# A hybrid decoder block with 32 experts: w_out in other ring slots, another order of the scan's units, half loads and half sums

## The chip, the cores and the metric

The kernel runs on 1 core of one Trainium2 chip. The metric is the device time of one execution in microseconds; the median of several is compared. All data is float32 unless a tile says bf16.

## The reference, cut to what matters

One layer on 256 tokens of width 1024. A norm and one wide projection feed a short convolution and an RWKV-7 scan; both are gated and merged, go through `w_out`, and a top-4-of-32 mixture of experts follows, then the last norm.

```python
p = rmsnorm(h, norm_mix_g) @ w_in                 # 1024 x 8480
y_conv = gb * conv3(gc * xin)
y_rwkv = rwkv7_time_mix(...)                      # 16 heads of 64, LoRA decay, head norms
h = h + (sigmoid(gate_conv) * y_conv + sigmoid(gate_rwkv) * y_rwkv) @ w_out
hn = rmsnorm(h, norm_ffn_g)
for e in experts:                                 # w1[e] 1024 x 2048, w2[e] 1024 x 1024
    h += gate_e * (clamped_swiglu(hn_e @ w1[e] + b1[e]) @ w2[e] + b2[e])
return rmsnorm(h, norm_final_g)
```

The scan is a recurrence over tokens of a 64 x 64 state per head with a decay, a rank-one removal and a rank-one addition per token. Heads' keys are normed: kk / max(|kk|, 1e-12).

## The kernel before, in words

**Memory.** `ring` has 16 slots of 2048 columns (1 MiB each). In the first part, slots 0 to 5 hold three double slots for chunks of `w_in` and `w_out` (`LOADS`, L251, gives the double slot of each of the 17 + 2 chunks), slots 6 to 10 K, KK, A, R and V, and 11 to 15 other arrays of the scan. The temporaries of the four lanes (64 tokens each) lie in `temps` (L125): one work array, slot 15, slot 4 and slot 5. In the expert part the ring is four groups of four slots (`GROUP`, L317). An expert takes three groups in turn: two for the halves of `exp_w1`, one for `exp_w2`, which is loaded in two halves.

**The queues.** SP (L374 on) issues the loads in program order. A chunk waits until the blocks of the chunk before it in its slot are projected (`blk_done`). An expert's loads (`load_expert`, L410) wait on `w_used`, which TensorE raises by 16 while it frees the slots of the first part (L862, L903, L910) and then by one for each slot used: 8 for `exp_w1`, 4 for `exp_w2` an expert. So an expert's first two groups wait for it * 12 + 4 and + 8, the halves of the third for + 10 and + 12. ACT issues the residual x (L1276) and some small loads.

**Order of work.** TensorE turns x (L459), projects blocks 0 to 66 (`project`, L480), each 8 x 2 records, and puts other work between blocks. In the first stage these are the LoRA products of the decay and of the in-context rate (`decay_and_iclr`, L498, after blocks 3 to 10), the head sums (`norm_sums`, L524, after block 11), their spread back over features (`norm_to_features`, L534, after block 13) and the gate's LoRA (L508). On VectorE the shift of each block (L1455), the prefix sum of the decay (L1479), its centring (L1488) and the norm's limit and reciprocal (L1490, L1494) stand in a fixed order.

From block 19 on comes the scan stage, an order written out by hand for TensorE (L742 to L859), ACT (L1189 to L1272) and VectorE (L1655 to L1789). The four lanes each build factors, invert a triangular matrix by a series and three merges (corner, joined, turn_e) and then pass through the state steps (z, u, y, s). `go` (L566) interleaves one or two units of 16 small products (64 x 64); a unit works either on the diagonal quadrants of the array or on the others, and `MERGE_AT` (L304) says which for the merges. Projections of the gates and of the convolution lie between, with copies, products and convolutions on ACT and VectorE (`gate_factor`, `take_gc`, `mix`, `convolve`, `gate_in`, `gate_conv`).

Then four out products (L866; t is the half of the tokens, half that of the columns), the turned residual for the router (L877), the choice of experts, and 32 experts (`expert`, L964): bias, eight slots of `exp_w1` (L983), the sum of the expert before (`combine`, L944), the gather for the next expert (L935), turns, four slots of `exp_w2` (L1018). At the end the last `combine`, the adds (L1898), and row by row the square sum and root on ACT (L1278), the reciprocal and the product with root and gain on VectorE (L1904), and the store (L443).

```python
pe.wait_ge(y_made, NCH)
pe.sem_inc(w_used, 8)
...
for n in range(NIN + 2):
    if n >= 3:
        sp.wait_ge(blk_done, blocks_until(buffer_before(n)))
```

Of the kernel before, what the change touches and what calls it, by code (L numbers as in the profile page):

```python
# [15 lines left out]
P = 128  # L16
# [62 lines left out]
def build(nc, x, w_in, w_out, norm_ffn_g, norm_final_g, w2, a2, g2, router_w, router_b,  # L79
          exp_w1, exp_b1, exp_w2, exp_b2, params, consts, out):  # L80
    with ExitStack() as ctx:
# [48 lines left out]
        gffn, gfin = flat(i_GB)[:, 1024:2048], flat(i_CS)[:, 0:1024]  # L130

# [18 lines left out]
        gfin_in = sem("gfin_in")  # L150
        merged = sem("merged")
# [99 lines left out]
        LOADS = [0, 1, 2, 0, 1, 2, 0] + [1, 0] * 6  # L251
# [52 lines left out]
        MERGE_AT = ((0, 1, 1), (1, 1, 0), (0, 0, 1), (0, 1, 0))  # L304
# [12 lines left out]
        GROUP = [8, 4, 12, 0]  # L317

        def group(u, j):

            return (3 * u + j) % 4
# [52 lines left out]
        def _(sp):  # L374
# [73 lines left out]
        def _(pe):  # L448
# [315 lines left out]
            go(series(0, 2), turn_v(0))  # L764
            go(f_rk(1), square(2))
            go(f_rb(2), series(1, 0))
            project(30)
            go(turn_e(0, 0), turn_b(0))
            go(series(2, 0), turn_v(1))
            go(series(1, 1), f_ak(2))  # L770
            go(turn_k(0))
            project(31)
            go(series(2, 1), f_rk(2))
            go(corner(0, 0), turn_b(1))
            project(32)
            go(turn_v(2), series(2, 2))
            go(turn_k(1), joined(0, 0))
            go(series(1, 2))
            go(turn_b(2), turn_e(2, 0))
            go(turn_e(0, 1))  # L780
            go(corner(0, 1))
            go(turn_k(2))
            project(33)
            go(joined(0, 1), corner(2, 0))
            go(turn_e(1, 0))
            go(corner(1, 0))
            go(turn_e(0, 2), joined(2, 0))
            project(34)
            go(joined(1, 0), turn_e(2, 1))
            go(corner(0, 2), corner(2, 1))  # L790
            project(35)
            go(joined(0, 2), joined(2, 1))
# [1140 lines left out]
```

## Time and profile before

| | us |
|---|---|
| median of 3 runs (lowest, highest) | 1344.51 (1344.16, 1347.29) |
| the profiled execution | 1345.06 |
| its span | 1343.3 |
| TensorE busy | 1234.8 (92%) |
| VectorE busy | 301.4 (22%) |
| ACT busy | 217.2 (16%) |
| GpSimd busy | 53.5 (4%) |
| DMA read, mean rate | 448.16 MB, 334 GB/s |
| chain that ended last | PE 63%, DMA 31%, DVE 3%, ACT 1%, issue 1% |
| waits of L983 for exp_w loads | 46.9 |

A span is the time from the first to the last record of the execution; what lies around it is 1.8 us here. Busy shares are means over stages with different limits: TensorE is busy nearly always, and its records in the expert part overlap with each other, so that share doesn't say that it sets the pace there. The chain follows each piece back to what released it. PE is TensorE's products, PEld its weight loads, DVE VectorE, POOL GpSimd. Line numbers are those of the kernel before.

### The profile page before, as it was taken

The numbers are of one execution on the slowest core, as the hardware profiler recorded it, in microseconds if no ns is written. First come the engines' busy times: TensorE is split into PE (matmuls) and PEld (weight loads), VectorE is DVE, ScalarE is ACT, GpSimd is POOL, SyncE is SP. The second block draws the span as 40 slices with busy tenths as digits, with TensorE's granted clock in tenths as the row PEclk, the third lists the DMA queues.
The fourth block names the chain that finished last, engine by engine and source line by source line (L and its number), as shares of the span: only waits on it lengthen the run. The fifth ranks groups of instructions, "written<-read, shape, count | busy, mean of one in ns | idle before, by whom it ended". The sixth has DMA issues, their size and how long they took to land.

```text
span 1343.3 us, 23536 instructions
## 1 busy us (share of the span) xinstructions
PE 1234.8 (92%) x10432; PEld 638.1 (48%) x10433; DVE 301.4 (22%) x597; ACT 217.2 (16%) x340; POOL 53.5 (4%) x32
## 2 busy tenths in 40 slices
PE   5989999999989999999999999899999989999996
PEld 4767888888744334333333333333333333343332
DVE  1254434233123112111112111111111111121112
ACT  4532221231032001100001100001110000110001
POOL 0700202000011000000000000000000000000000
PEclk9989999999988999999999999999999999999998
DMA  9421122333597999999999999999999999999993
GB/s 298 166 81 63 65 66 95 99 97 111 190 433 296 430 436 429 430 430 428 431 432 433 428 432 430 428 430 434 432 428 432 428 429 430 433 432 429 433 427 142
DMA packets 51620, 450.02 MB, mean 335 GB/s; under 512 B 5424, under 2 KB 23344, under 8 KB 35088
## 3 DMA queue, kind: packets, MB, share of 16 engines
q1 hardware_dynamic: 48576, 446.97, 80.0%
q10 hardware_dynamic: 2992, 2.25, 0.5%
q8 instruction: 46, 0.75, 0.2%
q14 instruction: 6, 0.05, 0.0%
HBM read 448.16 MB, written 1.05 MB: 334 GB/s over the span
## 4 chain that ended last, share of the span: by engine, by line
PE 63%; DMA 31%; DVE 3%; ACT 1%; issue 1%; ACTq 0%; SPq 0%; DVEq 0%
DMA ring<-in_exp_w 30%; PE ps L983 20%; PE ps L488 17%; PE ps L1018 10%; PE ps L573 4%; PE ps L949 3%; PE ps L940 2%; PE ps L873 2%; PE ps L575 1%; DMA ring<-in_w_out 1%; PE ps L996 1%; PE ps L973 1%; DVE work L1882 1%; PE ps L1005 1%; PE ps L506 0%
## 5 line engine op out<-in xcount | busy, mean ns | idle before, releaser
L983 PE MATMUL ps<-ring,work 128*64 128x512 f32 x2048 | 472.4, 617 | 46.9 <-DMA ring<-in_exp_w 46.9
L983 PEld LDWEIGHTS ps<-ring,work 128*64 128x64 f32 x2048 | 150.8, 142 | 351.2 <-issue 276.8
L488 PE MATMUL ps<-work,ring 128*128 128x256 f32 (+1 forms) x1120 | 244.1, 385 | 0.9 <-ACT work L1049 0.7
L1018 PE MATMUL ps<-ring,work 128*64 128x512 f32 x1024 | 225.1, 592 | 0.0
L488 PEld LDWEIGHTS ps<-work,ring 128*128 128x128 f32 (+1 forms) x1120 | 200.5, 186 | 34.6 <-issue 5.5
L1327 ACT ACTIVATE work<-work 128x512 f32<-128x512 f32 x32 | 20.1, 629 | 734.2 <-DVE work L1871 734.2
L1871 DVE TENSOR_SCALAR work<-ps 128x512 f32<-128x512 f32 x32 | 22.1, 692 | 500.0 <-PE ps L983 500.0
L1018 PEld LDWEIGHTS ps<-ring,work 128*64 128x64 f32 x1024 | 72.6, 137 | 129.5 <-issue 129.4
L1887 DVE COPY work<-ps 128x512 f32<-128x512 f32 x32 | 22.1, 691 | 208.2 <-PE ps L1018 208.2
L949 PE MATMUL ps<-work 64*128 64x512 f32 x264 | 65.6, 615 | 0.8 <-DVE work L1887 0.8
L940 PEld LDWEIGHTS ps<-sel,work 128*128 128x128 bf16 x1536 | 53.7, 118 | 24.2 <-issue 24.2
L940 PE MATMUL ps<-sel,work 128*128 128x64 bf16 x1536 | 57.1, 198 | 0.0
L573 PE MATMUL ps<-ring 64*64 64x64 f32 x1600 | 44.2, 220 | 2.1 <-issue 2.0
L949 PEld LDWEIGHTS ps<-work 64*128 64x128 f32 x264 | 22.8, 186 | 43.1 <-issue 41.5
L573 PEld LDWEIGHTS ps<-ring 64*64 64x64 f32 x1600 | 40.6, 135 | 4.9 <-issue 4.9
L1327 ACT ACT_TABLE_LOAD x32 | 41.1, 1283 | 2.1 <-issue 1.5
L873 PE MATMUL ps<-ring,work 128*128 128x512 f32 x64 | 30.0, 627 | 6.1 <-DMA ring<-in_w_out 6.1
L1329 ACT ACTIVATE work<-ps 128x512 f32<-128x512 f32 x32 | 19.1, 597 | 72.6 <-PE ps L940 72.6
L1005 PE MATMUL ps<-work,oh 96*64 96x512 bf16 x64 | 13.0, 403 | 16.5 <-DVE work L1882 16.5
L1461 DVE SCALAR_TENSOR_TENSOR ring<-ps,par,ring 128x255 f32<-128x255 f32 x24 | 11.5, 478 | 70.9 <-ACT ring L1066 70.7
L573 PE MATMUL ps<-cst,ring 64*64 64x64 f32 x768 | 25.2, 220 | 0.0
L1882 DVE COPY work<-ps 128x256 f32<-128x256 f32 x32 | 13.6, 424 | 50.8 <-PE ps L1000 50.8
(231 smaller groups left out, 733.0 us busy)
## 6 DMA issues: line engine op xcount, KB each, us to landing
ring<-in_exp_w SPq DMA_DIRECT2D x64, 4096.0 KB, 29.2
ring<-in_exp_w SPq DMA_DIRECT2D x64, 2048.0 KB, 30.0
ring<-in_w_in SPq DMA_DIRECT2D x8, 2048.0 KB, 8.3
ring<-in_w_in SPq DMA_DIRECT2D x16, 1024.0 KB, 6.7
ring<-in_w_out SPq DMA_DIRECT2D x2, 2048.0 KB, 10.3
ring<-in_w_in SPq DMA_DIRECT2D x1, 1152.0 KB, 7.3
work<-in_x SPq DMA_DIRECT2D x2, 512.0 KB, 4.1
work<-in_x ACTq DMA_DIRECT2D x2, 512.0 KB, 8.5
```

The source lines that it names most:

```text
L488: last = mm(bank_of(b)[width * g:width * g + width, 0:T], chunk(n)[:, k, c0:c0 + width], XN[:, k, :], start=k == 0, stop=k == KT - 1)
L573: last = mm(o, a(q, m), b_(q, m), start=True, stop=True)
L873: last = mm(ps[OUT[t][half]][:, :], Y[:, k, t * P:(t + 1) * P], chunk(NIN + half)[:, k, :], start=k == 0, stop=k == KT - 1)
L940: last = mm(ps[6][:, k * CAP:(k + 1) * CAP], H3[:, t, s, every_fourth(k)], sel[:, t, :], start=t + s == 0, stop=t + s == 3)
L949: last = mm(ps[2 * t + half][:, :], gts[64 * half:64 * half + 64, t * P:(t + 1) * P], yb[64 * half:64 * half + 64, :], start=False, stop=F ...
L983: last = mm(ps[4 + part][64 * half:64 * half + 64, :], xe[:, k * CAP:(k + 1) * CAP], ring[:, slot(u, k), part * D + half * 512:part * D + ...
L1005: last = mm(ps[7][64 * half:64 * half + 64, :], oh[:, :], b2s[:, half * 512:half * 512 + 512], start=True, stop=False)
L1018: last = mm(ps[7][64 * half:64 * half + 64, :], lhs, ring[:, slot(u, 8 + j), i * D + half * 512:i * D + half * 512 + 512], start=False, st ...
L1327: af(sig, glu, ACT.Sigmoid, scale=ALPHA).then_inc(sig_ready, 1)
L1871: ts(glu, ps[4][:, :], LIMIT, None, ALU.min).then_inc(glu_ready, 1)
L1882: cp(gts, ps[7][:, 0:T]).then_inc(gt_ready, 1)
L1887: cp(yb, ps[7][:, :]).then_inc(y_ready, 1)
```

## The change

Seven edits:
1. `w_out`'s two chunks go to slots 4, 5 and 2, 3 instead of 2, 3 and 0, 1. The first waits for the last merge of lanes 2 and 3, the second for chunk 15's blocks.
2. `GROUP` is [8, 12, 4, 0]; TensorE frees the second group when all four lanes are merged and the last two only after all four out products.
3. The table of the root is taken by a small root ahead of the first squares and ahead of the last ones; ACT's four small loads move behind the first root.
4. LoRA products in pairs; the norm's limit, ahead of the centring, and the root in block 11; shift(12) after the subtraction.
5. Another order of the units in the scan stage on three engines and another `MERGE_AT`; on GpSimd `first_e(2)` before `first_e(1)`. The same 118 units.
6. The second group of `exp_w1` of every second expert comes as two loads of two slots, each with a wait of its own.
7. The last sum is released per row half; the gain is multiplied ahead of the root, for one row on VectorE and for the other on GpSimd.

```diff
-        LOADS = [0, 1, 2, 0, 1, 2, 0] + [1, 0] * 6
+        LOADS = [0, 1, 2, 0, 1, 2, 0] + [1, 0] * 5 + [2, 1]
-        MERGE_AT = ((0, 1, 1), (1, 1, 0), (0, 0, 1), (0, 1, 0))
+        MERGE_AT = ((0, 1, 1), (0, 0, 0), (0, 1, 1), (0, 1, 0))
-        GROUP = [8, 4, 12, 0]
+        GROUP = [8, 12, 4, 0]
...
-                if n >= 3:
+                if n == NIN:
+                    sp.wait_ge(dve_e[2], 11)
+                    sp.wait_ge(dve_e[3], 11)
+                elif n >= 3:
                     sp.wait_ge(blk_done, blocks_until(buffer_before(n)))
...
+                    if (u, j) in half_in:
+                        rows_w1 = exp_w1[0, bass.ds(e, 1), 4 * P:8 * P, :].rearrange("a (p s) n -> p (a s) n", s=4)
+                        for half, done in ((0, group_in[group(u, j)]), (1, half_in[u, j])):
+                            sp.wait_ge(w_used, it * 12 + 6 + 2 * half)
+                            g0 = GROUP[group(u, j)] + 2 * half
+                            sp.dma_start(ring[:, g0:g0 + 2, :], rows_w1[:, 2 * half:2 * half + 2, :]).then_inc(done, 16)
+                        continue
...
-                if 3 <= b < 11:
+                if b in (4, 6, 8, 10):
+                    decay_and_iclr(b - 4)
                     decay_and_iclr(b - 3)
```

The scan stage on TensorE, its first third (the orders of ACT and VectorE follow it):

```diff
             project(23)
-            project(24)
-            project(25)
-            project(26)
             go(upper(0))
             go(lower(0))
+            project(24)
+            go(square(0), f_rb(0))
+            project(25)
+            go(upper(2), f_ak(0))
+            project(26)
+            go(f_rk(0), series(0, 0))
+            go(lower(2))
             project(27)
-            go(square(0))
-            go(upper(1), f_rb(0))
-            go(lower(1))
+            go(series(0, 1), f_rb(2))
+            go(turn_v(0), square(2))
+            go(upper(1))
+            go(lower(1), f_ak(2))
             project(28)
-            go(series(0, 0), f_ak(0))
-            go(upper(2), f_rb(1))
-            go(lower(2))
-            go(f_rk(0), square(1))
-            go(series(0, 1), f_ak(1))
+            go(square(1), f_rk(2))
+            go(series(2, 0), f_rb(1))
+            go(series(0, 2), turn_b(0))
...
```

Slots freed, the waits of an expert and the last sums:

```diff
             pe.wait_ge(y_made, NCH)
-            pe.sem_inc(w_used, 8)
+            pe.sem_inc(w_used, 4)
+            pe.wait_ge(merged, NCH)
+            pe.sem_inc(w_used, 4)
...
-            pe.wait_ge(merged, 4)
-            pe.sem_inc(w_used, 4)
             out_product(1, 0, 0, 8).then_inc(wout_done, 1)
...
             pe.wait_ge(wout_done, 2 * TT)
-            pe.sem_inc(w_used, 4)
+            pe.sem_inc(w_used, 8)
...
                 for k in range(8):
+                    if k == 6 and (u, 1) in half_in:
+                        pe.wait_ge(half_in[u, 1], turn_no * 16 + 16)
...
-            combine(n_rounds * E + 1)
+            pe.wait_ge(y_ready, n_rounds * E + 1)
+            for t in range(TT):
+                for half in range(2):
+                    last = mm(ps[2 * t + half][:, :], gts[64 * half:64 * half + 64, t * P:(t + 1) * P],
+                              yb[64 * half:64 * half + 64, :], start=False, stop=False, skip_group_check=True)
+                last.then_inc(last_sum, 1)
```

ACT, GpSimd and VectorE:

```diff
+            act.wait_ge(dve_chain, 1)
+            af(gn[:, 0, 0, 0:1], col[:, 31:32], ACT.Sqrt)
             for t in range(TT):
...
+            act.wait_ge(dve_rms, 1)
+            af(col[:, 4:6], col[:, 2:4], ACT.Sqrt).then_inc(act_rms, 1)
             mu_tail = P_AT["mu_lora"] + 2
             for g in range(4):
                 act.dma_start(col[32 * g:32 * g + 32, 40:41], params[0:32, mu_tail:mu_tail + 1],
                               allow_slow_non_contiguous=True).then_inc(mu_in, 16)
-            act.wait_ge(dve_rms, 1)
-            af(col[:, 4:6], col[:, 2:4], ACT.Sqrt).then_inc(act_rms, 1)
...
-                if b == 12:
+                if b == 11:
                     act.wait_ge(norm_max, 1)
                     af(nrm, nrm, ACT.Sqrt).then_inc(norm_root, 1)
...
+            af(gn[:, 0, 0, 0:1], col[:, 31:32], ACT.Sqrt)
             for t in range(TT):
                 root_of_squares(t, 16, 20, GC_rows, dve_h, 8 + t, act_h)
...
+            pool.wait_ge(dve_h, 9)
+            pool.wait_ge(gfin_in, 16)
+            ptt(HG[1], HB[:, 1, :], gfin, ALU.mult).then_inc(scaled_on_pool, 1)
...
-            shift(12)
             cs3 = flat(i_CS).rearrange("p (c t) -> p c t", t=HEAD)
-            link(tt(cs3, cs3, cm[:].rearrange("p m c -> p (m c)").unsqueeze(2).to_broadcast([P, NCH * KT, HEAD]), ALU.subtract))
             v.wait_ge(pe_sum, 1)
             ts(nrm, ps[4][:, 0:T], 1e-24, None, ALU.max).then_inc(norm_max, 1)
+            link(tt(cs3, cs3, cm[:].rearrange("p m c -> p (m c)").unsqueeze(2).to_broadcast([P, NCH * KT, HEAD]), ALU.subtract))
             link(tt(SW, CS, SW, ALU.subtract))
             v.sem_inc(dve_step, 1)
+            shift(12)
...
-            v.wait_ge(combined, n_rounds * E + 1)
+            v.wait_ge(gfin_in, 16)
             for t in range(TT):
+                v.wait_ge(last_sum, t + 1)
                 for half in range(2):
                     s_ = slice(512 * half, 512 * half + 512)
                     last = tt(HB[:, t, s_], HB[:, t, s_], ps[2 * t + half][:, :], ALU.add)
                 last.then_inc(dve_h, 1)
-            v.wait_ge(gfin_in, 16)
+            v.wait_ge(dve_h, 8)
+            link(tt(HG[0], HB[:, 0, :], gfin, ALU.mult))
             for t in range(TT):
                 v.wait_ge(act_h, 6 + t)
                 link(nc.vector.reciprocal(col[:, 22 + t:23 + t], col[:, 20 + t:21 + t]))
-                stt(HB[:, t, :], HB[:, t, :], col[:, 22 + t:23 + t], gfin, ALU.mult, ALU.mult).then_inc(out_ready, 1)
+                if t:
+                    v.wait_ge(scaled_on_pool, 1)
+                ts(HB[:, t, :], HG[t], col[:, 22 + t:23 + t], None, ALU.mult).then_inc(out_ready, 1)
```

## Rows read from the trace of the kernel before

**Rows 1.** Busy time by stretch: engines, then granted clock, DMA share, GB/s.

```profile
80.00:90.00 10.00, 7.43 (x36) 5.82 (x37) 4.87 (x4) 2.90 (x4) 0.00 (x0) 0.66 0.00 0
90.00:100.00 10.00, 9.24 (x46) 6.98 (x44) 5.81 (x11) 4.52 (x6) 0.00 (x0) 1.00 0.60 211
464.00:473.00 9.00, 9.00 (x48) 3.00 (x45) 0.89 (x2) 0.00 (x0) 0.00 (x0) 1.00 1.03 439
```

**Rows 2.** The timeline of the first norm: start, us, engine, line, idle before.

```profile
9.14 1.28 ACT L1046 ACT_TABLE_LOAD   x1 [2.16 <-issue]
...
10.67 0.17 DVE L1441 RECIPROCAL col<-col 128x2 f32<-128x2 f32 x1 [3.40 <-ACT col L1046]
...
10.87 1.42 DVE L1443 TENSOR_SCALAR ring<-work,col 128x1024 f32<-128x1024 f32 x2
```

**Rows 3.** The timeline of TensorE, the stage of the LoRA products and head norms.

```profile
31.73 0.70 PE L506 MATMUL ps<-work 64*128 64x256 f32 x4 [0.80 <-ACT work L1090]
...
71.04 7.07 PE L488 MATMUL ps<-work,ring 128*128 128x256 f32 x32
82.57 2.09 PE L540 MATMUL ps<-work,left 32*128 32x256 f32 x16 [4.46 <-DVE work L1494]
84.59 8.36 PE L488 MATMUL ps<-work,ring 128*128 128x256 f32 x32
```

**Rows 4.** The chain of waits in the scan stage: start, us, what.

```profile
204.29 2.02 PE ps L573 x128
...
225.97 1.09 PE ps L573 x64
227.07 3.65 PE ps L488 x16
```

**Rows 5.** The timeline of TensorE around the out products.

```profile
325.51 34.80 PE L488 MATMUL ps<-work,ring 128*128 128x256 f32 x160
...
373.23 15.93 PE L873 MATMUL ps<-ring,work 128*128 128x512 f32 x32 [6.05 <-DMA ring<-in_w_out]
...
389.87 7.03 PE L873 MATMUL ps<-ring,work 128*128 128x512 f32 x16
```

**Rows 6.** The timeline of VectorE around the head norms.

```profile
75.67 2.28 DVE L1488 TENSOR_TENSOR work<-work,cm 128x2048 f32<-128x2048 f32 x1
77.99 0.42 DVE L1490 TENSOR_SCALAR work<-ps 128x256 f32<-128x256 f32 x1
...
80.77 1.75 DVE L1494 RECIPROCAL work<-work 128x256 f32<-128x256 f32 x1 [0.15 <-DVE work L1491]
```

**Rows 7.** Who TensorE waited for up to 360 us: in total, times, longest.

```profile
PE ps L573 <- issue: 2.9, 4, 1.2
```

**Rows 8.** The timeline of SP: the first loads that wait for expert 0's end.

```profile
439.55 7.63 SPq L419 DMA_DIRECT2D ring<-in_exp_w  x2
```

**Rows 9.** The timeline of the last expert and the last norm.

```profile
1311.00 7.09 PE L983 MATMUL ps<-ring,work 128*64 128x512 f32 x32 [1.00 <-DMA ring<-in_exp_w]
...
1331.09 1.99 PE L949 MATMUL ps<-work 64*128 64x512 f32 x8 [0.80 <-DVE work L1887]
...
1333.13 2.48 DVE L1898 TENSOR_TENSOR work<-work,ps 128x512 f32<-128x512 f32 x4 [1.99 <-PE ps L949]
...
1335.61 1.28 ACT L1284 ACT_TABLE_LOAD   x1
...
1338.90 1.28 DVE L1904 SCALAR_TENSOR_TENSOR work<-work,col 128x1024 f32<-128x1024 f32 x1
```

**Rows 10.** DMA issues with us to landing: those of 420 to 421, of 439 to 440.

```profile
ring<-in_exp_w SPq DMA_DIRECT2D x1, 4096.0 KB, 13.6
...
ring<-in_exp_w SPq DMA_DIRECT2D x1, 4096.0 KB, 14.0
```

**Rows 11.** The timeline of GpSimd and VectorE while both work on SBUF.

```profile
405.46 2.13 POOL L1405 TENSOR_TENSOR left<-work 128x1024 f32<-128x1024 f32 x1 [6.44 <-DVE work L1843]
...
405.86 1.94 DVE L1848 SCALAR_TENSOR_TENSOR cnt<-cnt 128x1 f32<-128x1 f32 x2
```

More of the change, by code:

```diff
@@ L130, in build @@
         gffn, gfin = flat(i_GB)[:, 1024:2048], flat(i_CS)[:, 0:1024]
+        HG = (flat(i_CS)[:, 1024:2048], flat(i_GB)[:, 0:1024])
         const_in = sem("const_in")
@@ L766, in _ @@
[L766 removed]
+            go(turn_e(0, 0), turn_k(0))
+            go(f_ak(1), series(1, 0))
+            go(turn_v(2), series(2, 1))
             project(30)
[L768 to L771, printed above, removed]
+            go(corner(0, 0), turn_b(2))
+            go(series(2, 2), f_rk(1))
             project(31)
[L773 to L774 removed]
+            go(turn_v(1), joined(0, 0))
@@ L775, in _ @@
+            go(series(1, 1), turn_k(2))
             project(32)
[L776 to L782, printed above, removed]
+            go(turn_e(0, 1), series(1, 2))
+            go(corner(0, 1), turn_e(2, 0))
+            go(turn_b(1), corner(2, 0))
             project(33)
-            go(joined(0, 1), corner(2, 0))
@@ L802, in _ @@
+            project(38)
             go(joined(1, 2), f_ak(3))
-            project(38)
-            go(y_values(0), f_rk(3))
-            go(s_values(0), square(3))
-            go(z_values(0))
             project(39)
-            go(turn_v(3), series(3, 0))
-            go(u_product(0))
+            go(z_values(0), square(3))
+            go(s_values(0), y_values(0))
+            go(f_rk(3))
+            go(u_product(0), series(3, 0))
             project(40)
+            go(z_values(1), series(3, 1))
@@ L843, in _ @@
+            go(s_u(2))
+            project(53)
+            go(y_state(3), z_state(3))
+            project(54)
             go(u_product(3))
-            project(53)
+            project(55)
             go(y_u(3), turn_y(2))
-            project(54)
-            project(55)
             project(56)
-            go(turn_y(3))
             project(57)
@@ L1197, in _ @@
             scaled(19 + 4)
+            lower(0)
             scaled(19 + 5)
+            square(0)
             scaled(19 + 6)
             scaled(19 + 7)
-            lower(0)
+            lower(2)
             gate_factor(0)
-            square(0)
+            square(2)
+            turned(0, 0, V)
             lower(1)
@@ L1206, in _ @@
             square(1)
-            lower(2)
+            turned(0, 1, AA)
             gate_factor(2)
-            turned(0, 0, V)
-            square(2)
+            turned(0, 2, Kt)
+            turn_e(0, 0)
+            turned(2, 0, V)
             gate_factor(3)
-            turned(0, 1, AA)
-            turn_e(0, 0)
+            turned(2, 1, AA)
+            gate_factor(4)
             turned(1, 0, V)
-            turned(0, 2, Kt)
-            gate_factor(4)
+            turned(2, 2, Kt)
+            gate_factor(5)
+            turn_e(0, 1)
+            turn_e(2, 0)
             turned(1, 1, AA)
-            gate_factor(5)
-            turned(2, 0, V)
-            turned(1, 2, Kt)
-            turned(2, 1, AA)
-            turn_e(2, 0)
-            turn_e(0, 1)
-            turned(2, 2, Kt)
             gate_factor(6)
             turn_e(1, 0)
-            turn_e(0, 2)
+            turned(1, 2, Kt)
             gate_factor(7)
             turn_e(2, 1)
+            turn_e(0, 2)
             take_gc(0)
@@ L1233, in _ @@
             lower(3)
+            take_gc(1)
             turn_e(1, 2)
-            take_gc(1)
+            take_z(0)
             square(3)
-            take_z(0)
-            turned(3, 0, V)
             take_u(0)
@@ L1241, in _ @@
             square_y(0)
+            turned(3, 0, V)
+            root_y(0)
             turned(3, 1, AA)
-            root_y(0)
-            turned(3, 2, Kt)
             take_z(1)
@@ L1659, in _ @@
             shift(19 + 4)
+            upper(0)
+            lower(0)
             shift(19 + 5)
+            f_rb(0)
             shift(19 + 6)
+            f_ak(0)
+            upper(2)
             shift(19 + 7)
-            upper(0)
+            series(0, 0)
+            f_rk(0)
+            lower(2)
             v.wait_ge(hs_copied, 4)
```

180 lines of the change are left out of this document (87 added, 93 removed).

## The prediction

> **What bounds the kernel now.** I read the page first, then the chain of waits, then one stretch at a time by engine. The chain has two regimes. Up to expert 0 it is TensorE's own work, broken by a few waits. After that it runs through the loads of the expert weights: these keep the 16 DMA engines at about 430 GB/s and a full share, whichever weight is loaded (439 GB/s in a stretch of exp_w2) [rows 1]. 32 experts of 12.58 MB at that rate are 936 us, so most of the kernel can't be moved by reordering. What can move is what comes before the stream flows without gaps, and the tail after its last load. The stream holds only 16 slots. It fills once, then waits for expert 0 to use some. In that gap TensorE sets the time at which it resumes, so what TensorE gains ahead of expert 0 should reach the end one for one.
>
> **The first norm (ACT order and table).** Behind its squares (6.98) ACT issues four small DMAs (2.16 us) and then loads the table of the root (1.28 us) before the root itself can start, at 10.4, though VectorE had the mean ready 3.40 us before its next operation at 10.67, at 7.27 [rows 2]. After the change the table comes in while x is still on its way, and the DMAs stand behind the root: it starts at 7.3. All that follows is a chain into the transposes: 3.1 us won. The four DMAs are issued 0.5 us later and then take their 2.1 us of ACT's queue, which ends at 9.7; ACT's next work, the copies of the transposes, can't start before those scales of x (now 7.8 to 9.2) are turned. VectorE waits for them too, but shift(0) needs project(0) first.
>
> The Trainium skill (ScalarE: Activation LUTs, What ACT_TABLE_LOAD costs) adds about 1380 ns of drain to each load of 1283 ns. The trace differs: the load ends at 10.42 and VectorE has the root at 10.67. By the page this removal and the one in the tail would be worth 1.4 us more each.
>
> **LoRA in pairs.** TensorE waited 0.80 us for the sigmoids before its first LoRA product [rows 3]; now project(4) stands in between (3.6 us), so nothing is late there. Eight detours become four. A single projection in between costs 3.65 us, one of a row 34.80/10 = 3.48 [rows 4, 5], so each detour saved is worth 0.17: 0.7 us. Sum 1.5 us. The scan starts 0.6 us later, which fits before norm_sums ends.
>
> **Head norms ahead of the centring.** TensorE has two projections (7.07 us from 71.04, ending at 78.11) to cover the norm chain, but VectorE took the limit of the sums (0.42 us) only at 77.99, behind shift(12) and the centring of 2.28 us, and the reciprocal (1.75 us) at 80.77, so TensorE waited 4.46 us [rows 3, 6]. In the new order: sums done 71.2, limit to 71.7, root to 72.2 under the centring and the subtraction (2 x 2.28, to 76.2), shift(12) to 76.7, reciprocal to 78.5. TensorE waits 0.45 us instead of 4.46: 4.0 won. The two projections behind the wait then took 8.36 us where the two ahead of it took 7.07 [rows 3], and the granted clock of the stretch from 80 to 90 is 0.66, between its two levels of 1.2 and 2.4 GHz [rows 1]. Without the wait I take the fall away too: 1.3, and 0.1 less wait for gate_lora. Sum 5.4 us. ACT now waits for the limit inside block 11 with scaled(12) queued behind it, but that isn't due before 74.7.
>
> **The other unit order (scan stage).** I count units in the code. Each go() puts a diagonal and an off-diagonal unit on the array together, and a pair costs what a single costs: one go between projections is 1.09 us, two are 2.02 [rows 4], so 0.95 each and 0.15 a run. Before there are 69 gos (20 single) in 28 runs, after 65 (12 single) in 32 runs. 4 x 0.95 - 4 x (0.15 + 0.17) = 2.5 us less work. Waits between back-to-back gos were 2.9 us in 4 places [rows 7]. I followed each unit's operands through the new orders of VectorE and ACT: in most cases a projection stands between producer and user; the closest are turn_v(0) behind the bonus product and square(1) behind lower(1), with over 1 us to spare. I leave 0.3 us of waits: 2.6 won. Sum 5.1 us. Bounds: nothing (new waits eat the 4 gos; the orders of three engines moved at once) to 7.0.
>
> **w_out into the temporaries' slots.** The second half of w_out is loaded only after the last projection, beside the first two expert groups, and out_product(0, 1) waits 6.05 us for it. It then runs slowly: 15.93 us for two products, where one by itself takes 7.03, some 6.9 without the overlap at its ends [rows 5]. After the change its slots are those of chunk 15, free four projections (14 us) before the end; the first half goes to the temporaries of lanes 2 and 3 and is issued eight projections (28 us) before the end. At 350 GB/s (worked out below) its 2.1 MB need 6 us. SP's new wait for those two lanes is met when it gets there, since SP first waits for block 58. TensorE then goes through: from 360.3 four products and the turns between (0.7) are 28.3 us, against 36.6 (389.87 + 7.03 = 396.9). 8.3 won. The residual x, which ACT loads beside the expert groups, comes late for the first product as before, but its add is due only when the second product has ended, 7 us later.
>
> **Ring groups in another order.** The third group (exp_w2 of expert 0) and the fourth are now issued only after all four products, where the third had gone at 373.5. All above taken off (23.4), the products end at 373.5. Two groups of 4.19 MB need 22 us from there at 430 GB/s, to 396. Expert 0 was done at 439.55 [rows 8] and its exp_w2 calls are as many as one group of exp_w1 has, 7.09 us [rows 9], so they now begin at 409: hidden. Were that cover gone, it would cost at most the 13.6 us of a load on an empty queue [rows 10].
>
> **Half loads.** The refill is issued when expert 0 has used two slots instead of four: some 4 us sooner. But the load behind it and the two of exp_w2 waits until expert 0 is finished (439.55), and landed 14.0 us later, where the one issued on an idle queue took 13.6 [rows 8, 10]. So only 0.4 us reaches the stream; the rest becomes a gap. In the tail, TensorE waited just 1.00 us at the last expert's second group [rows 9]: the split gives that 1.0 and no more. Sum 1.4.
>
> **Sums per row half.** The first adds start behind two of the four calls, half of their 1.99 us sooner, and the table load of 1.28 us goes under the expert's work [rows 9]: row 0's root is ready 2.3 us sooner. VectorE then multiplies row 0 by the gain (1.28) while GpSimd does row 1 (2.13); each scale by the root is 0.71 (1.42 for two in the first norm) [rows 2]. Would they run side by side, the last scale ended 2.4 us sooner. But beside a GpSimd operation of 2.13 us two VectorE operations on one element each took 1.94 us, until GpSimd was done [rows 11]. VectorE's product starts first (from 1334.7 to 1336.0 on the old clock), so GpSimd's ends at 1338.1, and the last scale at 1338.9 instead of 1340.2: 1.3 won.
>
> The Trainium skill (SBUF — State Buffer, SBUF: two separate sides) says that a VectorE operation in a two-port mode, or with two SBUF inputs, and a GpSimd one lock each other out, whoever is first. The row agrees for two inputs; for a scale by a column no row shows it.
>
> **Sum.** 3.1 + 1.5 + 5.4 + 5.1 + 8.3 + 1.4 + 1.3 = 26.1 us. The profiled execution took 1345.06 (0.55 over the median of 1344.51), so 1319.0; the median of new runs may read half a microsecond lower.
>
> **The rivals.**
> Both scales wait for GpSimd: if row 0's scale is locked out like a two-input one, both run after 1338.1 and end at 1339.6: the tail gives 0.6, time 1319.7. This is the page's rule above.
> New waits in the scan stage: if the order loses what it saves in gos, 1324.1. For it: three orders interlock, and VectorE and ACT have table loads there. Against: the gaps of before stood where three and more gos followed each other, and there are fewer of those now.
> The w_out gain isn't passed on, because the two late groups hold up expert 0 or the stream: 1327.3. For: their issue moves behind the products. Against: 20 us of slack.
> More than forecast: no waits left in the scan (7.0) and a side-by-side tail (2.4): 1316.0.
> **Slower:** the halved loads read [p, 2, 2048] instead of one flat row. If they are cut in smaller pieces and run like w_in, 211 GB/s at a share of 0.60, so 350 at a full one [rows 1], the 67 MB of the 16 halved groups take 191 us instead of 156: +35 us, time 1354. It decides from 26 us on. Against: exp_w2's rows are half as long as exp_w1's and load as fast.
>
> **How the numbers follow.** Forecast 0.42, both scales wait 0.15, waits in the scan 0.20, w_out not passed on 0.08, more than forecast 0.10, slower 0.03, some mishap that leaves no difference 0.02. The range 1314.5 to 1328 takes in all cases that are faster, with 1.5 us below the best for clock falls that I priced too low. A measurement of this kernel tells 0.3% (4 us) from no change. Faster 0.95, same 0.02, slower 0.03.
>
> **What would show it.** Right: first transposes at 9.3; norm_to_features waits under 1 us; last projection ends near 345; no wait for in_w_out, and the four products take 28.3 us; expert 0 ends 23 us earlier, near 416; the refill's gap moves behind its w2 loads; no table load behind the last sums. Wrong: a stretch of halved loads under 420 GB/s, TensorE waits above 3 us between 130 and 300, or a second group of expert 0 or 1 that lands late.

## The result, and the profile after

| | us, median (lowest to highest) | profiled execution | its span |
|---|---|---|---|
| before | 1345.37 (1344.16 to 1347.29) | 1345.06 | 1343.3 |
| after | 1329.99 (1327.33 to 1332.31) | 1329.39 | 1327.6 |

The ratio is 0.9877, with an interval of 0.9863 to 0.9891: faster by 15.4 us, where 26.1 was forecast. The sign was right, the size was not: the time lies 2 us above the range.

To see where the gain went, I cut both traces at the same five events and compare the lengths of the pieces, in us.

| piece | before | after | won | forecast |
|---|---|---|---|---|
| start to the end of the head sums | 117.9 | 106.3 | 11.6 | 10.0 |
| scan, up to the first product of the output | 242.2 | 242.7 | -0.5 | 5.1 |
| the four products of the output | 36.8 | 34.2 | 2.5 | 8.3 |
| from there to expert 0 | 15.0 | 15.0 | 0 | 0 |
| expert 0 to the end of the last exp_w1 | 906.1 | 904.3 | 1.8 | 1.4 |
| the tail, to the end of the span | 25.2 | 25.0 | 0.2 | 1.3 |

Two pieces carry the miss. First the scan. The view of who TensorE waited for, from 104 to 365 us (in total, times, longest), after the change:

```profile
PE ps L588 <- issue: 5.5, 5, 2.2
```

It answers to [rows 7]: the saved gos are there, but there are 2.6 us more of waits that have no engine at their other end.

One pair of traces is a weak base for this. The traces of the experiments below include two more with the old order, and four more with the new order and nothing done against these waits: with all products of that window counted, the old order's waits on issue are 3.1 to 4.6 us (mean 3.9) in a scan of 242.2 to 243.6 (mean 243.0), the new order's 4.3 to 5.5 (mean 5.0) in one of 240.4 to 242.7 (mean 241.5). So the new order wins 1.5 us in the mean, not -0.5, still far from 5.1.

The longest wait, in the chain of waits of the changed kernel (start, us, what):

```profile
213.97 1.09 PE ps L588 x64
215.06 3.65 PE ps L502 x16
...
219.80 0.95 PE ps L590 x62
220.75 1.16 PE ps L588 x40
221.91 2.23 issue
224.14 1.76 PE ps L588 x54
225.90 4.32 PE ps L502 x16
```

The wait falls in the middle of a go, behind 40 of its small products, and the projection behind it takes 4.32 us where its neighbour takes 3.65. So TensorE does not seem to wait for an operand of a unit. What else moved just then shows in the view of the DMA engines from 205 to 230 us, in 40 slices (busy tenths, GB/s), with its queues:

```profile
DMA  0000000000000000779999999960000000000000
GB/s 0 0 0 0 0 26 0 0 0 0 0 0 26 0 0 0 75 224 370 388 378 369 352 349 347 342 185 0 0 0 0 0 26 0 0 0 0 0 0 0
q8 instruction: 4, 0.07, 1.0%
```

The lone slices of 26 GB/s are packets of the queue that the profile calls "instruction": 16 KB each, the lone ones 4 us apart or more. The load of w_in's chunk 11 fills the engines from 215 to 222 us, and the fourth such packet lies within it: in narrower windows it starts at 221.52 us and takes 1.07 us.

Second, the products of the output. The timeline of TensorE and of SP, after:

```profile
345.39 1.00 SPq L433 DMA_DIRECT2D ring<-in_exp_w  x2
...
349.02 20.76 PE L886 MATMUL ps<-ring,work 128*128 128x512 f32 x48
373.59 1.62 PE L896 MATMUL ps<-cst,work 128*128 128x128 f32 x8 [3.81 <-DVE work L1825]
375.00 8.23 PE L886 MATMUL ps<-ring,work 128*128 128x512 f32 x16
```

The 6.05 us for w_out of [rows 5] are gone: three products go through in 20.76 us. Then TensorE waits 3.81 us for the residual, and the last product takes 8.23 us; the granted clock from 374 to 376 us is 0.50, the lower of its two levels. VectorE had in turn waited for x, as the chain shows:

```profile
349.67 0.47 ACTq L1296
350.14 0.03 issue
350.17 22.06 DMA work<-in_x
372.25 1.30 DVE work L1825 x2
```

The DMA issues of the whole execution (KB each, us to landing) have x at 21.7 us:

```profile
work<-in_x ACTq DMA_DIRECT2D x2, 512.0 KB, 21.7
```

Before the change it was 8.5 us, and x was issued 0.3 us ahead of the expert groups, since SP had stood at w_out's second half until then (the same views of the kernel before):

```profile
346.53 14.18 SPq L391 DMA_DIRECT2D ring<-in_w_out  x2
360.81 1.03 ACTq L1276 DMA_DIRECT2D work<-in_x  x2
361.11 1.00 SPq L419 DMA_DIRECT2D ring<-in_exp_w  x2
...
work<-in_x ACTq DMA_DIRECT2D x2, 512.0 KB, 8.5
```

The tail, timeline of the last norm, answers to the end of [rows 9]:

```profile
1315.59 1.99 PE L1044 MATMUL ps<-work 64*128 64x512 f32 x8 [0.80 <-DVE work L1912]
...
1316.84 2.48 DVE L1924 TENSOR_TENSOR work<-work,ps 128x512 f32<-128x512 f32 x4 [1.20 <-PE ps L1044]
...
1319.40 3.26 POOL L1439 TENSOR_TENSOR work<-work 128x1024 f32<-128x1024 f32 x1 [918.32 <-DVE work L1924]
...
1320.69 2.52 DVE L1933 TENSOR_SCALAR work<-work,col 128x1024 f32<-128x1024 f32 x1
...
1323.31 0.75 DVE L1933 TENSOR_SCALAR work<-work,col 128x1024 f32<-128x1024 f32 x1
```

VectorE's scale of row 0 takes 2.52 us and ends 0.55 us after GpSimd's product; the same scale a moment later takes 0.75.

### The profile page after: what moved, and what is told of

Same layout as the page of the kernel before. It is cut to its first block, busy times and chain, and to the rows that moved or that the text cites. A ratio compares the mean times of both kernels' runs of the same rounds, so it can differ in the third digit from the quotient of the medians.

```text
span 1327.6 us, 23606 instructions
## 1 busy us (share of the span) xinstructions
PE 1223.7 (92%) x10433; PEld 642.8 (48%) x10433; DVE 304.0 (23%) x598; ACT 213.5 (16%) x339; POOL 58.9 (4%) x33
## 3 DMA queue, kind: packets, MB, share of 16 engines
HBM read 448.16 MB, written 1.05 MB: 338 GB/s over the span
## 4 chain that ended last, share of the span: by engine, by line
PE 62%; DMA 32%; DVE 3%; issue 1%; ACT 1%; SPq 0%; ACTq 0%; DVEq 0%
DMA ring<-in_exp_w 30%; PE ps L995 20%; PE ps L502 17%; PE ps L1030 10%; PE ps L588 4%; PE ps L959 3%; PE ps L950 2%; DMA work<-in_x 2%; PE ps L590 1%; PE ps L1008 1%; PE ps L983 1%; DVE work L1907 1%; PE ps L886 1%; PE ps L1017 1%; PE ps L1012 0%
## 5 line engine op out<-in xcount | busy, mean ns | idle before, releaser
L995 PE MATMUL ps<-ring,work 128*64 128x512 f32 x2048 | 465.1, 611 | 50.4 <-DMA ring<-in_exp_w 50.4
L995 PEld LDWEIGHTS ps<-ring,work 128*64 128x64 f32 x2048 | 159.0, 141 | 341.1 <-issue 286.8
L1030 PE MATMUL ps<-ring,work 128*64 128x512 f32 x1024 | 225.1, 592 | 0.0
L1030 PEld LDWEIGHTS ps<-ring,work 128*64 128x64 f32 x1024 | 72.5, 137 | 129.6 <-issue 129.5
L1439 POOL TENSOR_TENSOR work<-work 128x1024 f32<-128x1024 f32 x1 | 3.3, 3256 | 918.3 <-DVE work L1924 918.3
L1486 DVE SCALAR_TENSOR_TENSOR ring<-ps,par,ring 128x255 f32<-128x255 f32 x24 | 11.6, 482 | 60.2 <-ACT ring L1085 59.8
## 6 DMA issues: line engine op xcount, KB each, us to landing
work<-in_x ACTq DMA_DIRECT2D x2, 512.0 KB, 21.7
```

The lines of the kernel that those rows point to most:

```text
L995: last = mm(ps[4 + part][64 * half:64 * half + 64, :], xe[:, k * CAP:(k + 1) * CAP], ring[:, slot(u, k), part * D + half * 512:part * D + ...
L1030: last = mm(ps[7][64 * half:64 * half + 64, :], lhs, ring[:, slot(u, 8 + j), i * D + half * 512:i * D + half * 512 + 512], start=False, st ...
```

## The experiments

The theory after this reading had three parts. **x:** the expert groups, no longer behind w_out on SP, are issued 4 us ahead of x (345.39), and x, in 4 KB packets on ACT's queue, shares each DMA engine with their 32 KB packets. **Code:** TensorE runs dry of instructions where many small products follow one another, above all when a load has the DMA engines. **Tail:** VectorE is locked out by GpSimd. All ratios are to the kernel before, timed beside them (1345.8 to 1347.1 us); the changed kernel's was 0.9877 (0.9863 to 0.9891).

**1. Expert loads held until x has landed.**

```diff
+            sp.wait_ge(xres_in, 16 * TT)
             with sp.Fori(0, E // 4) as i:
```

> The changed kernel, but SP issues no expert load before the residual x has landed. Theory (x, issued on ACT's queue behind two expert groups already in flight, waits in each DMA engine behind their 32 KB packets): x lands within 6 us of its issue instead of 22, the four out products run through in 28.3 us instead of 34.1, and the time falls by 5.5 to 6 us to about 1324; the expert groups start some 9 us later, which costs nothing. Rival 1 (the x loads are slow by themselves, through their 4 KB rows or ACT's queue): x still takes some 20 us and the time does not move. Rival 2 (the expert stream is late already): the out products gain 5.8 us, but the first expert starts later or waits, and the time stays or grows.

1324.0 us (1322.55 to 1326.34), ratio 0.9825 (0.9805 to 0.9845). TensorE's timeline:

```profile
350.36 20.76 PE L887 MATMUL ps<-ring,work 128*128 128x512 f32 x48
370.96 1.04 PE L897 MATMUL ps<-cst,work 128*128 128x128 f32 x8
371.83 7.03 PE L887 MATMUL ps<-ring,work 128*128 128x512 f32 x16
```

x landed in 5.5 us, the wait and the slow product are both gone, and the four products take 28.5 us: the 28.3 of the prediction. The expert groups are issued 12 us later (357.80), where 9 was expected, and no wait for them comes of it: from the products to expert 0 it is 15 us in both traces.

**2. exp_w1 in pieces of 8 KB** (all its loads read "(s p)" instead of "(p s)", so the rows of W1 lie in another order and the output is another).

> The changed kernel with exp_w1 loaded in pieces of 8 KB instead of 32 and 16 KB (rows of exp_w1 so meet other features: the experts compute another sum, with the same amount of work). Theory (each packet of x waits for one expert packet on its engine): x has 16 packets of 4 KB per load and engine, 32 in all; with 8 KB packets of 0.3 us instead of 1.2 us it lands in 8 to 12 us instead of 22, soon enough for the second product, and the out products take 29 to 31 us. If x just shared the bandwidth by bytes, it would land at the same 22 us. The same kernel prices small pieces for the stream: if 8 KB pieces run as fast as 32 KB ones (430 GB/s), the expert stage stays at 904 us and the time falls by 3 to 6 us; if they cost 5%, 268 MB take 31 us longer.

1337.68 us (1336.0 to 1338.66), ratio 0.9929 (0.9909 to 0.995). With nothing held, x landed in 14.0 us and the products again took 28.5 us: how long x takes hangs on the size of the others' packets. That is later than the 8 to 12 us expected; x's two loads are 256 packets of 4 KB, so 16 for each engine and not 32. The price is in the stream, busy time by stretch (engines, clock, DMA share, GB/s), from 500 to 1200 us, first the changed kernel, then this one:

```profile
500.00:1200.00 700.00, 644.44 (x3964) 257.06 (x3960) 114.89 (x242) 73.67 (x96) 0.00 (x0) 0.98 1.00 430
```

```profile
500.00:1200.00 700.00, 636.04 (x3918) 255.17 (x3916) 113.86 (x240) 73.66 (x96) 0.00 (x0) 0.98 1.01 424
```

1.4% less, and the experts take 917.6 us instead of 905.8 in experiment 1. So the case of 430 GB/s and a gain of 3 to 6 us did not come.

**3. The load of chunk 11 held until block 41 of the scan.**

```diff
+                elif n == 11:
+                    sp.wait_ge(blk_done, 41)
                 elif n >= 3:
```

> The changed kernel, but the load of chunk 11 of w_in (214 to 222 us) is held until block 40 is projected. In the changed kernel TensorE stood 2.2 us at 221.9, within four gos in a row, with all operands there. Theory (its code is late: the gos use instructions faster than they are fetched, and the fetch shares the DMA engines with the load): the wait falls to 0.5 to 1 us, as at the other places without a load, the projection behind it runs at full clock, and the scan stage gets 1.5 to 2.5 us shorter. Rival (an operand or a semaphore): the wait stays at 2.2 us. If holding the chunk is too late, a wait for the ring appears before block 43 instead.

1327.8 us (1326.87 to 1329.25), ratio 0.9859 (0.9839 to 0.9879). The scan took 239.7 us instead of 242.7 (241.5 in the mean of the five traces above). By its time alone the gain is not clear of the noise, since the interval overlaps that of the changed kernel; the trace is clearer. Who TensorE waited for:

```profile
PE ps L590 <- issue: 3.2, 5, 1.4
```

The work and the order of the engines are the changed kernel's; only a load went elsewhere, and 2.3 us of waits with it. Between 205 and 240 us 0.5 us of them are left, of 2.2:

```profile
216.33 3.65 PE ps L504 x16
...
221.07 0.95 PE ps L592 x62
222.02 1.16 PE ps L590 x40
223.18 0.54 issue
```

TensorE stops behind the same 40 products, 6.85 us after the start of the same projection (216.33, in the changed kernel 215.06). But the instruction packet starts 4.80 us after it (221.13) instead of 6.46 (221.52): 1.66 us sooner without the load, and the wait is 1.69 us shorter. The packet itself takes as long, 1.12 and 1.07 us. Nor is it only this wait. In all 14 traces of this document, from the start of the small products to the products of the output, the chains have 71 waits on issue of over 0.15 us, and each of them ends 1.2 to 1.6 us after one of these packets has landed, while the packets themselves are mostly 4 us or more apart. The long wait stands in every trace of the new order in which nothing is done against it: 2.23, 2.23, 2.18, 2.18 and, on the kernel before, 1.95 us.

**4. The old scale at the end** (no product on GpSimd, VectorE's fused scale by root and gain as before; the half sums and the early table stay).

> The changed kernel with the last rows scaled as before (one VectorE operation of 1.28 us a row with root and gain, nothing on GpSimd), but sums per row half and the early table kept. Theory (GpSimd and VectorE lock each other out there, so the split of the scale costs more than it gives): from the last sums' first product to the end of the last scale 7.0 to 7.3 us instead of 8.5, and the time 1.2 to 1.5 us shorter. Rival (the tail is set by the stores): no gain.

1330.58 us (1328.12 to 1331.2), ratio 0.9872 (0.9851 to 0.9893): no difference that the median shows. In the trace the last norm is shorter:

```profile
1319.10 1.99 PE L1044 MATMUL ps<-work 64*128 64x512 f32 x8 [0.80 <-DVE work L1909]
...
1323.37 1.28 DVE L1926 SCALAR_TENSOR_TENSOR work<-work,col 128x1024 f32<-128x1024 f32 x1
...
1324.77 1.28 DVE L1926 SCALAR_TENSOR_TENSOR work<-work,col 128x1024 f32<-128x1024 f32 x1
```

From the last sums to the last scale 6.95 us, against 8.47 after and 9.09 before; the tail to the span's end 23.0, against 25.0. The tail is 23.0 to 23.1 us in all five traces with the old scale and half sums, and 25.0 to 25.1 in the five with the new one. What may hide it in the median is told with experiment 8.

**5. w_out's slots alone** (on the kernel before).

> The kernel before with one part of the change: both groups of w_out go into the temporaries' slots (with the ring groups in the other order and the wait of the loads that goes with them); norms, scan order, expert loads in 4 MB and tail stay as before. Theory (residual x is the limit once w_out is not): products of the output 34 us instead of 36.6, x 20 us or more from issue to landing, TensorE waits some 4 us for the centred residual, all together 1342.9 us. Rival 1 (the gain of 8.3 us that the prediction gave this part, x lands in time when nothing else is changed): products 28.3 us, 1337. Rival 2 (the part gives nothing by itself): 1345.4.

1344.43 us (1341.64 to 1346.94), ratio 0.9987 (0.9976 to 0.9999). x took 21.5 us, TensorE waited 3.61 us for the residual, and the products took 34.9 us: the late x comes with this part (w_out's place, the groups' order and their wait) and needs nothing else of the change. The time fell by 1.4 us against the kernel before beside it, half of the expected 2.9; this trace's head sums and scan are together 2.8 us longer than in the first trace of before, by the spread that is told above and with experiment 8.

```profile
362.97 20.76 PE L878 MATMUL ps<-ring,work 128*128 128x512 f32 x48
387.34 1.97 PE L888 MATMUL ps<-cst,work 128*128 128x128 f32 x8 [3.61 <-DVE work L1802]
389.10 8.77 PE L878 MATMUL ps<-ring,work 128*128 128x512 f32 x16
```

**6. The scan's order alone** (on the kernel before).

> The kernel before with another part of the change alone: the order of units, projections and sums in the scan, on all four engines. Theory (2.5 us of work are saved, but as much comes back as waits of TensorE with no engine late): scan from project 19 to the products of the output 242.4 to 243 us as before, TensorE idle on issue about 5.5 us in place of 2.9, 1345 to 1346 us together. Rival (the new waits belong to another part of the change, such as the other place of w_out): scan 240 us, idle on issue about 3, 1342.9 us.

1345.8 us (1342.57 to 1350.12), ratio 0.9994 (0.9979 to 1.0008). The time is as expected, the reason only in part: in the trace the scan was 1.8 us shorter (240.4), with 4.3 us of idle on issue, but w_out's second half, still loaded late, was waited for 6.20 us, and the products took 38.0 us instead of 36.8. So in this trace 1.3 us of the gain was lost again at the products; why they took longer than before is not shown.

**7. Projections 40 to 46 one place earlier** in TensorE's order (on the kernel after).

```diff
             go(s_values(0), y_values(0))
+            project(40)
             go(f_rk(3))
             go(u_product(0), series(3, 0))
-            project(40)
+            project(41)
             go(z_values(1), series(3, 1))
             go(y_u(0), s_u(0))
             go(turn_v(3))
-            project(41)
+            project(42)
...
```

> The kernel after, with projections 40 to 46 one place earlier in TensorE's order, so that the longest run of small products without a projection is cut in two. Theory (TensorE runs dry where a long dense run of small instructions uses up its code faster than it is brought, so a projection of 1.1 us or more within the run covers it): the wait of 2.2 us near 222 us goes or falls under 1, idle on issue 5.5 -> 3.5, about 1328 us. Rival (the code arrives late whatever stands there, the wait moves with it): idle on issue 5 or more, 1330 us. Other side: projection 40 stands before something that was ready earlier, 1331 to 1332 us.

1327.85 us (1324.76 to 1328.75), ratio 0.9859 (0.9833 to 0.9884). The chain over the same place, and who TensorE waited for:

```profile
220.47 0.95 PE ps L590 x62
221.42 3.65 PE ps L502 x16
225.07 2.01 PE ps L588 x94
227.08 3.65 PE ps L502 x16
```

```profile
PE ps L588 <- issue: 2.0, 5, 0.9
```

The load still runs beside it, and the wait is gone; the scan takes 238.6 us, 4.1 less than in the changed kernel's trace and 2.9 less than in the mean. The packet is no earlier, it runs from 222.18 to 223.24 us, but now the projection at 221.42 covers it. By the time alone this gain isn't clear of the noise either.

**8. Experiments 1, 3 and 4 together.**

> The kernel after with three edits together: expert loads held until the residual x has landed, the load of w_in's chunk 11 held until block 41 of the scan is done, and the old scale at the end (without GpSimd's product) with the new half sums. Theory (three separate places on the chain): from 1330.0 us, 6.0 less by the first as its own run showed, 1.5 to 2 less by the second, 1.5 less at the end (chain from the last sums to the last scale 6.95 us instead of 8.47): 1320.5 us. Rival (what one gives is taken back by the next, since expert 0's first groups then come late and the stream of 268 MB sets the end): 1323 to 1324 us.

1319.09 us (1317.28 to 1320.08), ratio 0.9793 (0.9771 to 0.9816). They add up: 28.5 us of products, 239.7 of scan, 23.0 of tail. That this is the prediction's 1319.0 is chance: the scan gives 2.5 of the 5.1 us forecast, and the tail and the experts give more than forecast.

All kernels with the new front fall into two groups: the head sums end at 106.3 to 106.8 us in six traces, at 108.3 to 109.0 in five. The source view of the first projections (ns shortest, median, longest) tells them apart only by the longest:

```profile
L502 PE MATMUL ps<-work,ring x60: 378/380/484, 13.4 to 21.8; 128*128 128x256 f32 x32, 128*32 128x256 f32 x28
```

```profile
L502 PE MATMUL ps<-work,ring x27: 379/379/796, 13.7 to 21.9; 128*128 128x256 f32 x27
```

The first is the changed kernel, the second experiment 4: some of its first products take 796 ns, twice the usual, at a granted clock of 1.00, and the first run of 128 projection products takes 20.3 us instead of 17.9. It is the slower by 2.0 to 2.4 us in 5 of the 11, and on the kernel before in one of three (experiment 5: 16.4 instead of 14.4 for 112 products). What decides it is open. Four executions don't average it out; that may be why the 2 us in the tail of experiment 4 don't show in its median.

**9 to 11. Further combinations:** all four edits; the same without the hold of chunk 11; all four with the halved loads whole again.

> The four edits that won something each, together: expert loads held for the residual x, chunk 11's load held, projections 40 to 46 one place earlier, old scale at the end. From 1319.1 us without the earlier projections. Theory (the hold of chunk 11 and the earlier projections cure the same wait near 222 us, so the second adds little to the first): idle on issue 2 us or less instead of 3.5, scan 238 to 239 us instead of 239.7, 1318 us. Rival (they cure different waits and add up): scan 236.5, 1316 us.

> As the combined kernel with the earlier projections, but chunk 11's load is not held. Theory: with a projection inside the run of small products the load beside it does no harm, scan 238.6 us as in the run that had the earlier projections alone, 1317.5 to 1318.5 us, same as with the hold. Rival (the load's share of the DMA engines costs something wherever code is fetched): 1320 us.

> As the combined kernel with the earlier projections, but the two halved groups of exp_w1 in every four experts are loaded whole again, in 4 MB. The prediction's theory for the halves (0.4 us from the refill, 1.0 us from the wait in the last expert, the stream at the same rate): 1.4 us slower than with halves, with a wait of 1 us for exp_w1's second group in the last expert. Rival 1 (the earlier refill counts whole, since the stream's one gap is 3.5 us shorter by it): 3.5 to 4.5 us slower. Rival 2 (32 more loads cost what they win): no difference.

| | us | ratio (interval) | scan | products | experts |
|---|---|---|---|---|---|
| all four | 1319.71 | 0.9796 (0.9782 to 0.9809) | 239.1 | 28.5 | 905.0 |
| no hold of chunk 11 | 1318.5 | 0.9783 (0.9769 to 0.9798) | 238.7 | 28.5 | 904.2 |
| loads whole | 1319.81 | 0.9802 (0.9789 to 0.9816) | 239.5 | 28.5 | 905.7 |

Their medians were expected at 1318, 1317.5 to 1318.5, and 1.4 us above the first. The hold and the earlier projections cure the same wait: together they give no more than the projections alone (238.6 of scan). The version without the hold beats both kernels, the one before by 2.2%; among the three and experiment 8 the intervals overlap. The halves are worth 0.7 us in this pair of traces, 1.3 if I take the mean of all eight traces with halves in 16 KB pieces (904.9) and of the five without (906.2), and too little for the medians, which leave the rival of no difference standing. With whole loads the wait at the last expert is back:

```profile
1287.89 7.09 PE L998 MATMUL ps<-ring,work 128*64 128x512 f32 x32 [1.02 <-DMA ring<-in_exp_w]
```

**12. The part ahead of the scan alone** (on the kernel before).

> The kernel before with the part of the change that lies ahead of the scan alone: the root's table first, the LoRA products in pairs, the limit of the norm sums ahead of the centring. The prediction's sum for it was 10.0 us; the changed kernel's trace showed the end of the head sums 11.6 us earlier in one pair of executions, and 10.7 in the mean over all traces taken. Theory (it reaches the end nearly one for one, since nothing after it has a fixed time): 1345.8 - 10.5 = 1335.3 us. Rival (what it wins is taken back at the products of the output, whose w_out is loaded at a time that other work sets): 1339 us or more.

1336.61 us (1334.89 to 1337.6), ratio 0.9921 (0.9907 to 0.9935): 10.5 us less than the kernel before beside it. It reaches the end one for one, as far as the noise lets one see. It waited 6.18 us for w_out, as before; that load is issued by TensorE's own progress, so it moves along.

## Why the prediction was wrong in size

**The front (forecast 10.0, was 11.6): right, a little small.** The first norm gave 3.1 and the norm wait 4.0, as worked out. The pairs of LoRA products gave 2.5 instead of 1.5: a pair with its two projections takes 8.17 us where two single ones took 8.56, so a detour saved is worth 0.4 and not 0.17, which I had as the difference of two numbers with three digits from other lines. The clock fall and its aftermath gave 2.1 instead of 1.4, since the products behind the wait that spread the norms back over the features ran slowly too (2.09 us in [rows 3], 1.15 now). The waits before the gate's LoRA stayed at 0.40 and 0.93 us, so the 0.1 for them didn't come. Both traces are of the quick kind of experiment 8.

**The other unit order (5.1, was -0.5): the term that failed is "I leave 0.3 us of waits".** The work saved was there: scan less waits is 2.6 us shorter in the means, where 2.5 was forecast. I had followed every operand and found over 1 us to spare, and no operand was late; but I took waits on "issue" for waits on operands that a better order removes. They grew from 2.9 to 5.5 us, and the projection behind the longest ran 0.7 us slower; that is about the whole miss in this pair of traces. In the means 1.5 us were won, and the miss of 3.6 us is again the waits: they should have lost 2.6 us and gained 1.1 (3.9 to 5.0). My rival "new waits in the scan" had the size, with the wrong mechanism; of its reasons, the table loads are ACT's alone (VectorE has none in the stage). Experiments 3 and 7 take the wait away in two ways that leave every operand's order alone: move the load, or put a projection into the run. What they leave is code that comes in 16 KB packets through the same DMA engines: the packet starts 1.66 us later beside the load and the wait grows by as much, and all 71 waits end 1.2 to 1.6 us after a packet. No view tells which instructions a packet brings, and why it starts late beside the load (in a queue, or asked for late) stays open. The prediction's own sign, waits of over 3 us between 130 and 300, came.

The Trainium skill (Runtime: NRT & Kernel Launch, Instruction fetch mechanics) states that an engine's instructions come in blocks of 16 KiB over a DMA queue of the sequencer's own, and that the cost is mostly hidden. The trace agrees on the block (46 packets, 0.75 MB) and not on the cost in this stage: up to 2.23 us at a time, 5.5 in all.

**w_out (8.3, was 2.5): the step that failed is "the residual x ... comes late for the first product as before, but its add is due only when the second product has ended, 7 us later".** That holds only if x lands as fast as the 8.5 us of before. But then SP was held at w_out until x was on its way; taking that hold off let two groups of 4 MB in front of it. x landed 23 us after the first product's start, the turn behind the third product waited 3.81 us, and the pause brought the clock down: 1.62 for 1.04 and 8.23 for 7.03. 34.2 less 28.5 is the 5.7 that is missing. I had looked at what the new place does to w_out and to the groups, and not at the third party on the same engines. Experiment 1 gives all of it back.

The Trainium skill (DMA: Bandwidth & Descriptors, Queues, rings and completion order) states that a DMA engine takes turns between its queues packet by packet. The runs agree: x took 21.7 us beside 32 KB packets, 14.0 beside 8 KB ones and 5.5 ahead of them. It is the rule that I should have weighed here.

**The tail (1.3, was 0.2): the rival was right.** From the last sums to the last scale it gave 0.6, as "both scales wait for GpSimd" had it: the scale of row 0 took 2.52 us beside GpSimd, 0.75 alone. GpSimd's product took 3.26 us, not 2.13; VectorE's product by the gain was under way when it started and ran on for 1.05 of the 1.13 us more. From the last scale to the end of the span another 0.4 was lost (3.5 us for 3.1): the two stores were issued 0.9 us apart instead of 1.4 and took 2.9 us to land instead of 2.7; that the one comes of the other is not shown. Worse, the second engine was a loss, not a small gain: with VectorE alone the tail is 2.0 us shorter, so the half sums and the early table won 2.2 and GpSimd gave it back.

The Trainium skill (SBUF — State Buffer, SBUF: two separate sides) states that of a VectorE operation in a two-port mode or with two SBUF inputs and a GpSimd one, whichever starts first holds the shared port pair for the whole instruction. The trace agrees for two inputs (GpSimd's product behind VectorE's); it adds that the scale by a column waited as well.

**Halves (1.4, was 1.8 in this pair of traces, 0.7 in another, 1.3 in the means) and the order of the groups (0):** right in size, as far as the traces tell. The refill came early and became a gap (a DMA share of 0.72 from 424 to 427 us), the 1.0 us wait is gone, and the late exp_w2 groups were hidden (two groups take 19.5 us at 430 GB/s, not the 22 of my sum, which changes nothing). The slower rival fell: the stream ran at 430 GB/s with pieces of 16 KB.

Taken together: 26.1 - 5.6 - 5.8 + 1.6 - 1.1 + 0.4 is 15.6; the spans differ by 15.7. The range failed for a reason of its own: I priced each rival alone, "waits in the scan" at 1324.1 and "w_out not passed on" at 1327.3, and its upper end of 1328 had no room for two of them together.

## What to carry to other kernels

When a wait is taken off a queue, list every transfer that the wait had kept apart, also those of other engines' queues: here one wait of SP had protected a 1 MB load whose delay cost 5.7 of 8.3 us, and one line that brings the protection back was worth as much. A wait "on issue" inside a run of small matrix products need not be an operand that is late: look for instruction packets that land just before it ends, spread larger instructions between the small ones, and keep loads away. And a second engine may be no help beside the first when both work on SBUF, as in this tail; time the pair before giving it work.

## What the runs showed that I had not expected

TensorE can run dry in the middle of a go of 64 x 64 products (0.2 to 2.2 us at a time). After the 2.23 us it works at the lower clock for a while: the granted clock from 224 to 226 us is 0.50, and a product takes 794 ns that takes 380 else. In 6 of 14 traces the first projections lose 2.0 to 2.4 us to such slow products although the granted clock is 1.00 throughout. And pieces of 8 KB cost 1.4% of the rate of a stream (424 for 430 GB/s), where 16 and 32 KB don't differ: with every group of exp_w1 in 32 KB pieces it is 431, with half of the second groups in 16 KB pieces 430.
